# The low part of a weight slab on GpSimd: four operations of 256 columns in place of two of 512

## What is computed

```python
mod = silu(c) @ w_ada + b_ada
sh1, sc1, g1, sh2, sc2, g2 = split(mod, 6)
h = x * (1.0 + sc1) + sh1
mix, ... = mixer_block(h, ...)            # h @ w_in, three mixers, @ w_out
x = layer_norm(DEEPNORM_ALPHA * x + g1 * mix, ln1_g, ln1_b)
h2 = x * (1.0 + sc2) + sh2
f = square(relu(h2 @ w_up)) @ w_down
x = layer_norm(DEEPNORM_ALPHA * x + g2 * f, ln2_g, ln2_b)
```

## Time and profile before

| | |
|---|---|
| median of 3 runs | 2097.32 us (2093.06 to 2099.24) |
| the profiled execution | 2099.51 us, its span 2097.6 us |
| PE busy | 2044.4 us (97%) |
| POOL busy | 1440.9 us (69%) |
| DVE busy | 1436.7 us (68%) |
| ACT busy | 908.0 us (43%) |

### The profile page before, as it was taken

How to read it: one execution, slowest core, us unless ns; L and a number is a source line. 1 busy time by engine, 2 the same in 40 slices (tenths; PEclk the granted TensorE clock), 3 DMA queues, 4 the chain that set the end, 5 groups by cost and what they waited for, 6 DMA issues and landing times.

```text
span 2097.6 us, 27969 instructions
## 1 busy us (share of the span) xinstructions
PE 2044.4 (97%) x10451; PEld 1713.2 (82%) x10451; DVE 1436.7 (68%) x1875; ACT 908.0 (43%) x1306; POOL 1440.9 (69%) x1101
## 2 busy tenths in 40 slices
PE   7899999999999999999999999999999999999996
PEld 5677887888997888888878888878888889999994
DVE  2455687696675545677887667788757777765686
ACT  2324213222213654545564554565444645444441
POOL 3345787874343677788878778887788866666672
PEclk9999999999999999999999999999999999999998
DMA  8796798873432455545445645544654534454341
GB/s 272 220 299 225 229 278 235 233 249 95 151 104 91 157 173 162 181 145 164 141 141 179 208 156 164 167 131 131 222 190 141 175 111 122 146 180 143 120 141 45
DMA packets 319953, 357.50 MB, mean 170 GB/s; under 512 B 12357, under 2 KB 251970, under 8 KB 319819
## 3 DMA queue, kind: packets, MB, share of 16 engines
q1 hardware_dynamic: 319818, 355.72, 54.4%
HBM read 321.22 MB, written 34.44 MB: 170 GB/s over the span
## 4 chain that ended last, share of the span: by engine, by line
PE 70%; DVE 8%; ACT 1%; POOL 1%; issue 1%; DVEq 0%; ACTq 0%
PE ps L1184 23%; PE ps L1186 22%; PE ps L1185 22%; PE ps L1448 1%; POOL w_hilo L897 1%; DVE hid_b L1911 1%; PE ps L1520 0%; DVE pair_sums L1933 0%; DVE pair_sums L1934 0%; DVE pair_sums L1930 0%; DVE htmp L1788 0%; DVE hid_a L1911 0%; DVE pair_sums L1929 0%; DVE mix L1628 0%; DVE acc L1783 0%
## 5 line engine op out<-in xcount | busy, mean ns | idle before, releaser
L897 POOL TENSOR_TENSOR w_hilo<-w_raw,w_hilo 128x512 fp32r<-128x512 f32 x890 | 1281.2, 1469 | 595.3 <-ACT w_hilo L978 594.5
L978 ACT ACTIVATE w_hilo<-w_raw 128x1024 fp32r<-128x1024 f32 x445 | 470.4, 1058 | 535.7 <-PE ps L1186 412.0
L1184 PE MATMUL ps<-hA,w_hilo 128*128 128x512 f32 (+1 forms) x1760 | 622.5, 354 | 9.3 <-ACT htmp L1054 4.1
L1185 PE MATMUL ps<-hA,w_hilo 128*128 128x512 f32 (+1 forms) x1760 | 620.3, 352 | 0.0
L1186 PE MATMUL ps<-hA,w_hilo 128*128 128x512 f32 (+1 forms) x1760 | 620.1, 352 | 0.0
L1184 PEld LDWEIGHTS ps<-hA,w_hilo 128*128 128x128 f32 x1760 | 332.0, 189 | 55.1 <-issue 8.4
L1185 PEld LDWEIGHTS ps<-hA,w_hilo 128*128 128x128 f32 x1760 | 332.0, 189 | 41.8
L1186 PEld LDWEIGHTS ps<-hA,w_hilo 128*128 128x128 f32 x1760 | 332.0, 189 | 41.5
L2007 DVE TENSOR_TENSOR acc<-acc,ps 128x512 f32<-128x512 f32 x270 | 177.9, 685 | 70.9 <-PE ps L1186 67.9
L1184 PE MATMUL ps<-w_hilo,hid_a 128*128 128x512 f32 x450 | 181.0, 402 | 1.7 <-ACT more_sums L1154 1.7
L1929 DVE TENSOR_TENSOR pair_sums<-htmp 128x256 f32<-128x256 f32 x62 | 36.2, 584 | 207.8 <-ACT htmp L1057 207.5
(11 more groups left out here) (239 smaller groups left out, 2830.4 us busy)
## 6 DMA issues: line engine op xcount, KB each, us to landing
w_raw<-in_w_up SPq DMA_DIRECT2D x128, 512.0 KB, 4.1
w_raw<-w_mix SPq DMA_DIRECT2D x124, 512.0 KB, 3.3
w_raw<-in_w_down SPq DMA_DIRECT2D x97, 512.0 KB, 3.8
w_raw<-in_w_in SPq DMA_DIRECT2D x64, 512.0 KB, 5.0
xt<-in_w_ada SPq DMA_DIRECT2D x20, 1024.0 KB, 8.4
w_raw<-in_w_out SPq DMA_DIRECT2D x32, 512.0 KB, 4.7
xt<-x_norm SPq DMA_DIRECT2D x19, 512.0 KB, 5.7
xt<-in_w_down SPq DMA_DIRECT2D x36, 256.0 KB, 5.0
```

The source lines that it names most:

```text
L897: ins = pool.tensor_tensor(W[:, g % SLOTS, 1, cols], raw[:, g % RAW, cols], W[:, g % SLOTS, 0, cols], ALU.subtract)
L978: act.activation(W[:, g % SLOTS, 0, :], raw[:, g % RAW, :], ACT.Copy).then_inc(hi_done, 1)
L1184: pe.matmul(out, w_hi, x_hi, start=start, stop=False)
L1185: pe.matmul(out, w_hi, x_lo, start=False, stop=False)
```

## The change

`lo_part` makes the 1024 columns of a slab's low part in four operations of 256 columns, where it made them in two of 512. Q is 256, HALF is 512. What is waited for and when `lo_done` is signalled stays: before the first operation, and with the last.

```diff
             def lo_part(g):
                 pool.wait_ge(hi_done, g + 1)
-                for half in range(2):
-                    cols = slice(HALF * half, HALF * half + HALF)
+                for part in range(4):
+                    cols = slice(Q * part, Q * part + Q)
                     ins = pool.tensor_tensor(W[:, g % SLOTS, 1, cols], raw[:, g % RAW, cols],
                                              W[:, g % SLOTS, 0, cols], ALU.subtract)
                 ins.then_inc(lo_done, 1)
```

## The result

| | before | after |
|---|---|---|
| median, measured side by side, 8 runs each | 2094.71 us (2092.37 to 2099.24) | 2100.62 us (2099.78 to 2103.59) |
| the profiled execution | 2099.51 us | 2101.61 us, its span 2099.7 us |

The change makes the kernel slower: the ratio is 1.0029 with a 95% interval of 1.0020 to 1.0037, 5.9 us, which is just within the 0.3% that the prediction counted as the same. The forecast was 3.4 us faster. The time lies inside the range, but the sign is wrong. The forecast of 2093.9 us also started from a median of 3 runs, 2097.32 us, that was 2.6 us above the median of 8; the change it gave is off by 9.3 us. The two profiled executions are only 2.1 us apart, because that of before was 4.8 us over its median; so the traces have to be compared stretch by stretch.

A forecast was written before the change was run, and what follows sets the result against it. PE, busy for 97% of the span, was taken as the bound, so only its waits could be won; -0.6 - 0.9 - 0.3 - 0.5 - 1.1 = -3.4 us from 2097.32 gave 2093.9 us, range 2087 to 2104.

The forecast's parts named there:

- POOL's cost of a slab: Low part alone: 2.76 us a slab in place of 2.50, +0.26 us on 445 slabs, 116 us of POOL's time.
- the slower rival: Steady blocks: at 0.81 us an operation a slab costs +0.74 us, POOL becomes the bound, about 2109 us; chance 0.12.
- The cover of the steady blocks: Some 2.6 us of cover against 0.26 us a slab, so the edit costs and wins nothing there.
- The gate sites: 1058 to 1066 and 1391 to 1399 us, around gate_acc: 0 at each, between -1.3 and +1.1 us.
- The Trainium skill: Gate sites: exclusive port lock for whole instructions would end each 2 us later, making the sum about +0.6; not followed.
- 326 us: Transposes at 324 us and the x load after: the load takes back DVE's gain; 0, between -1.3 and +0.5 us.
- 57 us: PE's wait on DVE hA: a DVE subtraction loses less to short POOL operations; -0.6 us, between -0.6 and 0.
- 467 us: Transposes with no late load behind: DVE's mixer chain meets cheaper slabs; -0.9 us, between -1.0 and 0.
- 595 us: PE's wait on L1817 (0.8 us): two or three DVE operations meet POOL; -0.5 us, between -0.8 and 0.
- 544 us: Start of the last mixer group, wait named "issue" (1.4 us): -0.3 us, between -0.6 and 0.
- 74 us: PE's wait on ACT gs (2.9 us) behind tiny DVE rsqrt operations: 0, between -0.6 and +0.3 us.
- 1697 us: ACT htmp wait (4.1 us): L1933 and L1934 each some 0.55 us shorter; -1.1 us, between -1.5 and +0.3.

The follow-up runs named there:

- e2: Kernel before with four 256-column operations in the MLP's slabs only, two of 512 in slabs 0 to 95: 2100.83 us beside 2095.76, ratio 1.0021.
- e6: Kernel before with each slab's low part in four operations of 504, 8, 504 and 8 columns: 2107.58 us, ratio 1.0056.
- e4: Kernel before with four 256-column operations only at the 27 slabs around gate_acc (blocks 9, 17, 25): 2100.96 us beside 2095.76, ratio 1.0023.
- e5: Kernel before with the loop rewritten but left at two pieces, the same program: 2094.84 us beside 2095.74, ratio 0.9998.
- e10: Kernel before with four 256-column operations only for slabs 48 to 95 and nine around the third gate_acc: 2091.99 us beside 2096.68, ratio 0.9979.
- e12: Kernel before with four pieces at slabs 48 to 95 and the third gate_acc, and DVE gating token tiles 1 and 0: 2087.39 us beside 2095.29.
- e9: Kernel before with one 1024-column operation per slab at the 27 slabs around gate_acc: 2102.49 us beside 2096.68, ratio 1.0029.

## Why the prediction was wrong, point by point

**POOL's cost of a slab** was taken as +0.26 us; rows give 2.54 to 2.83, +0.29. The bound of 0.81 us for an operation, on which the slower rival rested, is refuted. But the term that counts is the cost beside DVE. Over all 445 slabs POOL's low parts were busy for 1281.2 us and are for 1494.1, +0.48 a slab; in the 250 us without a wait, 27.7 us where I had 18. What is over 0.29 a slab is DVE's toll: a chain of DVE operations gets one in at each gap, and a slab now has four. I counted the shorter wait as DVE's gain and forgot that POOL pays for every meeting whatever its own operation's length.

**The cover of the steady blocks** held: no new wait and, from slab 90 to 185, not 0.01 us lost, though the distance between the end of the slab of the earlier trace rows and PE's need shrank from 2.8 to 2.5 us.

**The gate sites are the step that failed,** by the price of POOL's slabs around gate_acc. I wrote 0 each, between -1.3 and +1.1; they cost 3.3 and 3.4 us, 6.7 of the table. Slab 196 was to end between 1065.0 and 1067.4 us and ended at 1066.7, but that is luck: PE was 2.9 us ahead in the trace of after. Relative to PE the slab came 3.3 us later than before, outside the bounds of -1.3 and +1.1, and in e2, where PE is 3.8 us ahead, it is 3.4 later. Two terms of the sum failed:
- "Four slabs and gate_acc ahead of it start it 0.5 us late." At the end of the second gate_acc POOL was 2.6 us late relative to PE. I had priced those slabs at 0.26 us each, without a toll; slabs 189 to 191 alone took 13.2 us in place of 9.4, 1.3 more each, and 1.5 us were lost already before them.
- The five slabs behind it were to take 13.8 us and a toll of 3.6 to 6.0, 17.4 to 19.8 in all. They took 19.9, at the upper end, because the idle stretch closed and each operation of DVE found a gap.

Over the eight slabs the cost is 0.95 us a slab where I had 0.26, and slabs 192 to 194, which had 2.8 to 3.1 us of cover before PE needs them, have less than none. I had looked at slab 196 alone, the one that was late before. That DVE's operations moved onto those three slabs is seen in the trace, but e6 loses as much in waits without it. The slower rival named the right mechanism, POOL as the bound, and the wrong place: it looked for it in the steady blocks and priced it by a slab's cost alone, when in 39 us around gate_acc 4.9 us of slack was all there was.

**The Trainium skill,** "SBUF — State Buffer", section "SBUF: two separate sides", which I weighed there, speaks of an exclusive lock that blocks the loser for a whole instruction. By that rule the sum would have been +0.6, nearer in sign than mine. Its price is still too high for the traces: the residual of 1024 columns that met short operations took 1.65 us, 0.42 over its 1.23, where the wait for a whole POOL operation would be 0.70.

**326 us** was 0, between -1.3 and +0.5. The direction of the reasoning was right (the load takes back what DVE wins, because the combination stands behind POOL's slabs), its size wrong: POOL has almost no idle time there as well. The kernels with four equal pieces in that group lose some 2.7 us more than those with two (the mean of +3.2, +4.8, +2.8 and +3.4, less that of the eight others, +0.8). Part of it is clock, since after had 0.66 from 331 to 336 us and before 1.00; against the four kernels with two pieces and a slow stretch there (+2.1) it is 1.5 us more.

**57 us:** the DVE operation that met POOL fell from 1.63 to 1.11 us, as said, and the wait is gone; but it is also absent from e4, e5 and e10 to e12, which have 512 columns there, so the gain can't be told from variation. **467 us:** gone, as forecast (-0.9); it was also absent in e5 and e9, so it is worth less than that on average. **595 us:** 0.8 to 0.4, forecast -0.5. **544 us:** unchanged, forecast -0.3. **74 us:** unchanged within what varies.

**1697 us:** 4.1 to 2.8, forecast -1.1. The size is right by luck, since the operations are not the ones that I named. L1934 fell from 1.37 to 0.84 us as said, but L1933 stayed at 1.53, and the larger part came from the chain's first operation, L1929, which I had left to gate_acc. gate_acc starts 0.4 us later relative to PE there, which probably shortened that meeting; I had feared that it would add one. Before and after:

```profile
1691.89 1.37 DVE L1929 TENSOR_TENSOR pair_sums<-htmp 128x256 f32<-128x256 f32 x1 [3.82 <-ACT htmp L1057]
```

```profile
1695.62 0.51 DVE L1929 TENSOR_TENSOR pair_sums<-htmp 128x256 f32<-128x256 f32 x1 [3.00 <-ACT htmp L1057]
```

**The sum.** Gate sites +6.7, 326 us +1.5 to +2.7, 467 us about -0.7, 595 us -0.5, 1697 us -1.5 to -3.2 (with or without the slow clock behind it): +3.8 to +6.7, and 5.9 was measured. The two signs of e10, which keeps only the last three, and e4, which keeps mostly the first, bear it out.

## What to carry to other kernels

Splitting an operation on an engine whose operations and another's lengthen each other, as POOL's and DVE's do here, is a trade: the other engine waits less, and this one pays a fixed part for every piece and a toll for every meeting, of which there are now more. Decide it by stretch, not for the whole kernel: short pieces where the other engine's chain is what PE waits for, long ones where this engine has no idle time in a window of tens of microseconds, whatever its mean share. Where it has none, price its work with the toll of every meeting, from the first slab of the stretch on, and check all the results due there, not only the one that was late before. And compare times of two traces relative to the engine that bounds them: a lead from elsewhere can hide a loss.

## What the runs showed of the hardware that was not expected

- An 8-column operation of POOL is far from free: 0.19 us at least, and e6, with two of them and two of 504 in a slab, kept POOL as busy (1647.7 us) as four of 256 (1649.8).
- DVE gets its operations in one for each of POOL's in a chain: 2.5 us each against operations of 1024 columns, 1.40 against 512 (L1934's median), 0.85 against 256, where one is 0.43 alone.
- The stretches at 1.2 GHz stood at other places in nearly every trace: after had them at 331, 1392 and 1703 us among others, before at 544 and 1701, e10 none between 100 and 2000 us. The one at 1392 us lasted 3.4 us, which costs PE 1.7 us. A single pair of traces can therefore differ by several microseconds for a reason that the edit has no part in.
